# Two projection chunks finished ahead of the scan's norm, pads cleared on GpSimd, norm products between the convolutions

## The chip, the cores and the metric

One core of one Trainium2 chip runs the whole program. The time is the device time of one execution in microseconds (us). A few-word map of the engines in the profile: PE is TensorE (PEld its weight loads), DVE is VectorE, ACT is ScalarE, POOL is GpSimd, SP is SyncE, which issues most of the large loads. All arithmetic is fp32; a matmul with fp32 operands appears in the trace as two matmul instructions.

## What is computed

The reference is two layers of a diffusion backbone over 128 context tokens and 256 latent tokens, width 1024. Layer 0 runs a bidirectional state-space scan beside a gated long convolution (Hyena), layer 1 attention; each is followed by a mixture of 32 experts. The part that matters here is the junction of the two halves of layer 0:

```python
    y, final = bidirectional_ssd(xs, dt_raw, Bm, Cm, A_log, dt_bias, init_state)
    y = y + xs.astype(jnp.float32) * d_skip.astype(jnp.float32)[:, None]
    y = y.astype(h.dtype).reshape(b, L, SSD_INNER)
    y = rmsnorm(y * jax.nn.silu(z), g_ssd)
    parts = jnp.split(dwconv_centred(hy, hy_conv_w, hy_conv_b), 1 + HY_ORDER, axis=-1)
    filters = hyena_filters(L, hy_w1, hy_b1, hy_w2, hy_b2, hy_w3, hy_freq)
    u = parts[0]
    for o in range(HY_ORDER):
        u = parts[o + 1] * long_conv(u, filters[:, o], hy_bias[o])
    return jnp.concatenate([y, u], axis=-1) @ w_out, final
```

`y` is the output of the scan; its norm is over all 1024 channels. `hy` is a projection of 3072 channels, on which a depthwise convolution of three taps is run.

## The kernel before

**Layout and order.** Activations lie with channels on the 128 partitions and 384 tokens (128 + 256) along the row, so 1024 channels are 8 tiles, called chunks. The program has no automatic scheduler: each engine has its own instruction list written by hand, and the engines meet through semaphores. PSUM has 8 banks. The function `bank_plan` (from line 125) lists every bank's use in TensorE's order, with the engine that empties it; `bank_order` deals out the banks in rotation; and `open_bank` (line 840 on) makes TensorE wait until the earlier user of a bank has been emptied. `full(engine, name)` is the other direction: the engine waits until TensorE has completed that entry of the plan. Because both are counts along one list, moving an entry in the plan moves it in all lists.

**The end of the scan.** The scan has 12 steps (`QUADS`). Each ends with a `y` bank, which VectorE (lines 2203 and 2206) adds the skip term to and multiplies into `szT`. To fill TensorE's waits in the scan, the helper `hy_ahead` already issues 14 of the 16 contraction steps of the first two Hyena chunks, (0,0) and (0,1), which sit in banks 7 and 6 and lack only their last contraction step.

**After the scan, in each engine's order:**

- ScalarE squares the 8 chunks of `szT` into `sqssd` (line 1749), waits for TensorE's sum, takes its square root into `rstd` (`root`, line 1592), computes the second set of conditions (`conditions(1)`, line 1641, after the semaphore `const`), and then copies each Hyena chunk from its bank into `hpad`, a row with zero pads, in two pieces (lines 1766 and 1767). There are two `hpad` rows, so chunk c waits for the convolution of chunk c-2 (semaphore `hconv`). The first copy waits for the semaphore `hpad0`, the clearing of the pads.
- TensorE adds up the squares with a matrix of ones (`sum_squares`, 8 matmuls, each after its square), then issues the last contraction step of (0,0) and (0,1), then (0,2), then the filters' first small matmul `f` 0 (which waits for eleven small parameter loads, semaphore `hyc_in`), then (0,3). By the plan's rotation (0,3) uses bank 6, that is the bank of (0,1), which ScalarE must have copied out. Then come two column blocks of the conditioning matrix (`ada`, line 882), (0,4) to (0,6), and so on up to 24 chunks.
- VectorE waits for the root, inverts it (line 2213), forms the 8 norm products `szT` times gain times `rstd` (line 2215, semaphore `yn`), clears the second condition tile (line 2217) and `hpad` (line 2218), and then runs the 24 convolutions (lines 2244, 2245, 2247), with the argument reduction of the filters' sines (`filter_args`, lines 2230 to 2236) after chunks (0,2) and (0,6).
- GpSimd waits for the last `y` bank and issues eleven parameter loads for the filters (lines 2597 to 2604), which go through its own DMA queue, and then nothing until much later.
- SyncE issues the 2 MB weight blocks into a ring of 6 slots; each waits for TensorE's last use of the slot's former block (line 723).

The norm products are read late: ScalarE waits for `yn` before it uses `rstd` for something else, at the last conditioning block (line 1633), and TensorE in `first_states`, in the first turn of the long convolutions.

Of the kernel before, what the change touches and what calls it, by code (L numbers as in the profile page):

```python
# [114 lines left out]
def bank_plan():  # L115
# [3 lines left out]
    def job(name, by, block=None, bank=None):  # L119
        j.append((name, by, block, bank))  # L120
# [42 lines left out]
    for step in range(-1, len(QUADS)):  # L163
# [16 lines left out]
        if step in OFF_AFTER:  # L180
            for g in range(2):
                job(("off", *OFF_AFTER[step], g), "dve")
    job(("ss", "ssd"), "act")

    for q in range(3):
        for c in range(KD):
            job(("hy", q, c), "act", ("hy", q, c // 4) if c % 4 == 3 else None, FILL_BANK[c] if (q, c) in ((0, 0), (0, 1)) else None)
            if ("hy", q, c) in F_AFTER:
                job(("f", F_AFTER[("hy", q, c)]), "dve")
            ada_after(("hy", q, c))  # L190
            if ("hy", q, c) == FILTERS_AFTER:
                for i, (s, x, t) in enumerate(HY_FILTERS):
                    job(("PQ", *HYO[0], s, x, t), "act", None, (7, 6, 1)[i % 3])
            if (q, c) == GATES_AFTER:
                job(("gr", 0), "act")
                job(("gr", 1), "act")
# [228 lines left out]
def build_kernel(nc, A, K, outs):  # L425

    with ExitStack() as ctx:
# [204 lines left out]
        def full(eng, *name):  # L632

            eng.wait_ge(done, JOB[name] + 1)
# [9 lines left out]
        def bank(*name):  # L644
            return banks[BANK[JOB[name]]]
# [192 lines left out]
        def _(pe):  # L838
# [259 lines left out]
            for step in range(-1, len(QUADS)):  # L1098
# [9 lines left out]
                    chunk_state(STATE_AFTER[step])  # L1108
                if step in OFF_AFTER:
                    state_terms(*OFF_AFTER[step])  # L1110
            sum_squares("ssd", sqssd, KD)


            def product(t, h, k):
                act_at = szT[:, k, cols(t)] if k < KD else hyT[:, k - KD, cols(t)]
# [75 lines left out]
            for q in range(3):  # L1191
                for c in range(KD):
                    if c % 4 == 0:
                        arrived(("hy", q, c // 4))
                    if q == 0 and c < 2:
                        open_bank("hy", 0, c)
                        mm(bank("hy", 0, c)[:, 0:T], block_view(("hy", 0, 0))[:, KD - 1, c * P:(c + 1) * P], hT[:, KD - 1, :], False, True)\
                            .then_inc(done, 1)
                    else:
                        project(("hy", q, c), block_view(("hy", q, c // 4)), c % 4 * P, hT)  # L1200
                    if F_AFTER.get(("hy", q, c)) == 0:
                        pe.wait_ge(S("hyc_in"), 16 * 11)
                        ps = open_bank("f", 0)
                        mm(ps[0:HY_HID, 0:T], w1t[0:HY_FEAT, :], featt[0:HY_FEAT, :], True, True).then_inc(done, 1)
                    if F_AFTER.get(("hy", q, c)) == 1:
                        ps = open_bank("f", 1)
                        pe.wait_ge(S("fsin"), 1)
                        mm(ps[:, 0:T], w2t[0:HY_HID, :], h1[0:HY_HID, :], True, True).then_inc(done, 1)
                    ada_after("hy", q, c)
                    if ("hy", q, c) == FILTERS_AFTER:  # L1210
                        pe.wait_ge(S("hs"), 1)
                        pe.wait_ge(S("hypar0_in"), 16 * 6)
                        filters(0, *HYO[0])
                    if (q, c) == GATES_AFTER:
                        for l in range(2):
                            ps = open_bank("gr", l)
                            took(pe, "ada", l, 11)
                            for i in range(4):
                                g, v = divmod(i, 2)
                                last = tr(ps[0:KD, cols(i)], mod[:, l, 16 + 24 * g:24 + 24 * g, v])  # L1220
                            last.then_inc(done, 1)
# [349 lines left out]
        def _(act):  # L1571
# [175 lines left out]
            took(act, "y", NT - 1, 3)  # L1747
            for k in range(KD):
                A_(sqssd[:, k, :], szT[:, k, :], ACT.Square).then_inc(S("sq"), 1)
            root("ssd", D)  # L1750

            def take_filters(turn, b, o):
# [4 lines left out]
            act.wait_ge(S("const"), 2)  # L1757
            conditions(1)
            for c in range(3 * KD):
                if c == 0:  # L1760
                    act.wait_ge(S("hpad0"), 1)
                if c >= 2:
                    act.wait_ge(S("hconv"), c - 1)
                full(act, "hy", c // KD, c % KD)
                ps = bank("hy", c // KD, c % KD)
                A_(hpad[:, c % 2, 1:1 + LP], ps[:, 0:LP], ACT.Copy)
                A_(hpad[:, c % 2, 2 + LP:2 + T], ps[:, LP:T], ACT.Copy).then_inc(taken["act"], 1)  # L1767
                if ("hy", c // KD, c % KD) in F_AFTER:
                    i = F_AFTER[("hy", c // KD, c % KD)]
                    act.wait_ge(S("farg"), i + 1)  # L1770
                    dst = h1[0:HY_HID, :] if i == 0 else hsP
                    src = farg[0:HY_HID, :] if i == 0 else farg
                    A_(dst, src, ACT.Sin).then_inc(S("fsin"), 1)
                ada_after("hy", c // KD, c % KD)
                if ("hy", c // KD, c % KD) == FILTERS_AFTER:
                    act.wait_ge(S("gates_out"), 16 * 2)
                    take_filters(0, *HYO[0])
                if (c // KD, c % KD) == GATES_AFTER:
                    for l in range(2):
                        full(act, "gr", l)  # L1780
                        A_(gstage[0:KD, l, :], bank("gr", l)[0:KD, :], ACT.Copy).then_inc(taken["act"], 1)
                    took(act, "gr", 1)
                    for l in range(2):
                        act.dma_start(gates_d[l].rearrange("g v (c p) -> c (g v) p", p=P),
                                      gstage[0:KD, l, :].rearrange("c (i p) -> c i p", p=P)).then_inc(S("gates_out"), 16)
# [206 lines left out]
        def _(dve):  # L1992
# [218 lines left out]
            took(dve, "y", NT - 1, 3)  # L2211
            took(dve, "ss", "ssd")
            link(nc.vector.reciprocal(rstd, rstd))
            for k in range(KD):
                STT(out=szT[:, k, :], in0=szT[:, k, :], scalar=col("ssd_norm", k), in1=rstd, op0=mult, op1=mult).then_inc(S("yn"), 1)

            nc.vector.memset(conds[1], 0.0).then_inc(S("const"), 1)
            nc.vector.memset(hpad, 0.0).then_inc(S("hpad0"), 1)
            two_pi_hi = float(np.float32(6.28125))
            two_pi_lo = 2.0 * math.pi - two_pi_hi  # L2220
            magic = 12582912.0
# [17 lines left out]
            for c in range(3 * KD):  # L2239
                q, k = divmod(c, KD)  # L2240
                took(dve, "hy", q, k)
                src, acc = hpad[:, c % 2, :], hacc[:, c % 2, 0:n]
                dst = (u0T, p1T, hyT)[q][:, k, :]
                link(TS(acc, src[:, 0:n], col("hy_conv_w", c), col("hy_conv_b", c), mult, add))  # L2244
                link(STT(out=acc, in0=src[:, 1:1 + n], scalar=col("hy_conv_w", 3 * KD + c), in1=acc, op0=mult, op1=add))
                for v, (a, b) in enumerate(SEGS):
                    last = STT(out=dst[:, a:b], in0=src[:, 2 + a + v:2 + b + v], scalar=col("hy_conv_w", 6 * KD + c),
                               in1=acc[:, a + v:b + v], op0=mult, op1=add)
                last.then_inc(S("hconv"), 1)
                if ("hy", q, k) in F_AFTER:  # L2250
                    filter_args(F_AFTER[("hy", q, k)])
                ada_after("hy", q, k)
                if (q, k) == (2, 3):
                    gain(1, 0, "norm_ffn", 32, 11)
                    gain(2, 1, "norm_mix", 8, 11)
                    gain(3, 1, "norm_ffn", 32, 11)
                    dve.wait_ge(S("fsin"), 2)

                    nc.vector.memset(hsP[HY_HID:P, 0:1], 0.0)
                    link(nc.vector.memset(hsP[HY_HID:P, LP:LP + 1], 0.0))  # L2260
                    TS(hsQ, hsP, sgn[:, 0:1], None, mult).then_inc(S("hs"), 1)
# [307 lines left out]
        def _(pool):  # L2569
# [23 lines left out]
                    .then_inc(S("m2"), 1)  # L2593

            full(pool, "y", 2, 3)
            with nc.allow_non_contiguous_dma(reason="a few small parameters"):
                dma(dft, K["k_dft"]).then_inc(S("hyc_in"), 16)
                dma(w1t[0:HY_FEAT, :], A["hy_w1"][0]).then_inc(S("hyc_in"), 16)
                dma(featt[0:HY_FEAT, :], K["k_feat"]).then_inc(S("hyc_in"), 16)
                for j in range(2):  # L2600
                    dma(w2t[0:HY_HID, j * HY_HID:(j + 1) * HY_HID], A["hy_w2"][0]).then_inc(S("hyc_in"), 16)
                for src, c, n in ((A["hy_b1"][0], 0, 1), (A["hy_freq"][0, 0], 1, 1), (A["hy_b2"][0], 2, 2), (A["hy_freq"][0, 1], 3, 2)):
                    for j in range(n):
                        dma(fpar[j * HY_HID:(j + 1) * HY_HID, c:c + 1], src.rearrange("(p o) -> p o", o=1)).then_inc(S("hyc_in"), 16)
# [176 lines left out]
```

## Time and profile before

| | us |
|---|---|
| median of 3 runs | 1398.87 (1397.15 to 1399.19) |
| the profiled execution | 1394.66 |
| its span, first to last instruction | 1392.7 |
| TensorE busy | 1229.0 (88%) |
| VectorE, ScalarE, GpSimd busy | 458.3, 330.3, 190.3 |
| mean granted TensorE clock | 0.950 of full |

The profiled execution took 1394.66 us, 2.0 us more than its span and 4.2 us less than the median of the runs. Start times in the rows further down are counted from the span's start. An entry such as `[2.76 <-ACT arena L1767]` means that the engine stood idle for 2.76 us ahead of this instruction and that the instruction of line 1767 on ScalarE released it. A busy time of merged instructions can overlap the next row by a fraction of a matmul, because matmuls are pipelined.

### The profile page before, as it was taken

Reading aid. Unit: us, or ns where it says so; the run is one execution under the profiler, and the core shown is the slowest. Engines: PE = TensorE matmul, PEld = TensorE weight load, DVE = VectorE, ACT = ScalarE, POOL = GpSimd, SP = SyncE. Lnnn points to the kernel's source line nnn. Section 1 sums busy time; section 2 is a strip of 40 time slices with the busy share of each in tenths; the row PEclk is TensorE's granted clock in tenths of the full one; section 3 lists DMA queues with packets and bytes.
Section 4 is the critical chain, followed back from the end, with each engine's and each line's share of the span. In section 5 each row is a group of like instructions: output and inputs, shape, how many; then the busy total and the mean of one; then the engine's idle time right before and its main releaser. Section 6 shows DMA issues by size and latency. Waiting matters only on the chain.

```text
span 1392.7 us, 16599 instructions
## 1 busy us (share of the span) xinstructions
PE 1229.0 (88%) x6381; PEld 694.0 (50%) x6381; DVE 458.3 (33%) x960; ACT 330.3 (24%) x843; POOL 190.3 (14%) x251
## 2 busy tenths in 40 slices
PE   4999998899989999959999875999888959999774
PEld 2456654455545554446555442753455446555431
DVE  1452078533238850251111113212374241111115
ACT  4112364210022200131111113314353231111113
POOL 1000021100122401011221110152001011112100
PEclk9999999999999999979999997899999979999996
DMA  9895510475920108349999995941312469999993
GB/s 341 318 386 197 181 31 1 179 283 207 363 83 1 61 12 332 120 172 367 419 417 418 420 413 208 372 53 14 136 62 101 183 229 403 418 419 419 419 379 150
DMA packets 94418, 337.25 MB, mean 242 GB/s; under 512 B 12784, under 2 KB 16598, under 8 KB 69649
## 3 DMA queue, kind: packets, MB, share of 16 engines
q1 hardware_dynamic: 73472, 303.18, 55.6%
q0 software_dynamic: 13984, 26.19, 6.7%
q10 hardware_dynamic: 6897, 6.97, 1.5%
q8 instruction: 46, 0.75, 0.2%
q14 instruction: 19, 0.16, 0.0%
HBM read 334.08 MB, written 23.18 MB: 257 GB/s over the span
## 4 chain that ended last, share of the span: by engine, by line
PE 71%; DMA 16%; DVE 6%; ACT 3%; issue 2%; POOL 0%; SPq 0%; ACTq 0%; DVEq 0%; POOLq 0%
PE bank L851 63%; DMA ring<-in_moe_w_down_dram 10%; PE bank L855 5%; DMA ring<-in_moe_w_up_dram 3%; PE bank L882 3%; DMA arena<-expert_rows 1%; DMA xR<-in_x_sample_dram 1%; PE bank L948 1%; ACT ring L1958 1%; DMA hT<-rows,scr 0%; ACT rstd L1598 0%; DVE arena L2471 0%; DVE arena L2474 0%; DMA expert_rows<-arena,scr 0%; DVE arena L2498 0%
## 5 line engine op out<-in xcount | busy, mean ns | idle before, releaser
L851 PE MATMUL bank<-ring,arena 128*64 128x256 f32 (+3 forms) x2624 | 438.5, 439 | 43.6 <-DMA ring<-in_moe_w_up_dram 17.2
L851 PEld LDWEIGHTS bank<-ring,arena 128*64 128x64 f32 (+1 forms) x2624 | 218.3, 146 | 229.8 <-issue 119.9
L851 PE MATMUL bank<-hT,ring 128*128 128x384 f32 (+5 forms) x968 | 310.2, 479 | 7.0 <-ACT hT L1670 3.6
L851 PEld LDWEIGHTS bank<-hT,ring 128*128 128x128 f32 (+1 forms) x968 | 182.9, 196 | 130.1 <-issue 21.1
L851 PE MATMUL bank<-arena 128*64 128x256 f32 (+7 forms) x800 | 117.9, 385 | 10.4 <-DVE arena L2419 4.5
L2446 DVE TENSOR_TENSOR hT<-hT,bank 128x256 f32<-128x256 f32 x32 | 13.5, 421 | 265.8 <-ACT hT L1845 265.8
L851 PEld LDWEIGHTS bank<-arena 128*64 128x64 f32 (+4 forms) x800 | 60.4, 151 | 52.7 <-issue 30.2
L855 PEld LDWEIGHTS bank<-cst,hT 128*128 128x128 f32 x368 | 47.4, 190 | 47.8 <-issue 35.9
L1845 ACT ACTIVATE hT<-bank 128x256 f32<-128x256 f32 x32 | 12.3, 384 | 247.5 <-PE bank L851 247.5
L855 PE MATMUL bank<-cst,hT 128*128 128x128 f32 x368 | 61.0, 301 | 11.1 <-DMA hT<-rows,scr 11.1
L855 PE MATMUL bank<-cst,arena 128*128 128x128 f32 (+3 forms) x207 | 33.3, 312 | 37.5 <-ACT arena L1611 20.0
L851 PE MATMUL bank<-ring,hT 128*128 128x512 f32 x144 | 63.3, 598 | 0.4 <-ACT hT L1972 0.4
L851 PE MATMUL bank<-arena,ring 128*128 128x256 f32 (+3 forms) x272 | 60.0, 373 | 3.2 <-ACT arena L1921 1.8
L2451 DVE COPY arena<-bank 128x512 f32<-128x512 f32 x32 | 22.1, 691 | 111.4 <-PE bank L851 111.4
L851 PEld LDWEIGHTS bank<-arena,ring 128*128 128x128 f32 (+2 forms) x272 | 41.5, 184 | 23.9 <-issue 9.2
L855 PEld LDWEIGHTS bank<-cst,arena 128*128 128x128 f32 (+3 forms) x207 | 27.7, 162 | 48.3 <-issue 39.9
L851 PE MATMUL bank<-arena,cst 128*128 128x512 f32 (+5 forms) x76 | 37.8, 653 | 13.9 <-DVE arena L2392 9.4
L1856 ACT ACTIVATE arena<-bank 128x512 f32<-128x512 f32 x32 | 19.1, 597 | 114.4 <-PE bank L851 114.4
L851 PEld LDWEIGHTS bank<-ring,hT 128*128 128x128 f32 x144 | 27.5, 193 | 34.3 <-issue 33.2
L2667 POOL DMA_INDIRECT hT<-rows,scr x32 | 33.0, 1030 | 70.7 <-PE bank L855 26.8
L2683 POOL COPY scr<-arena 128x1 int32 x28 | 5.1, 183 | 270.5 <-ACT arena L1856 164.2
L2244 DVE TENSOR_SCALAR arena<-arena,par 128x385 f32<-128x385 f32 x24 | 11.6, 482 | 91.4 <-ACT arena L1767 91.4
(305 smaller groups left out, 1141.5 us busy)
## 6 DMA issues: line engine op xcount, KB each, us to landing
ring<-in_moe_w_up_dram SPq DMA_DIRECT2D x28, 2048.0 KB, 20.8
ring<-in_moe_w_down_dram SPq DMA_DIRECT2D x28, 2048.0 KB, 20.0
ring<-in_w_ada_dram SPq DMA_DIRECT2D x24, 2048.0 KB, 14.6
ring<-in_moe_w_gate_dram SPq DMA_DIRECT2D x24, 2048.0 KB, 20.8
ring<-in_ev_w_in_dram SPq DMA_DIRECT2D x11, 2048.0 KB, 11.5
arena<-in_moe_w_gate_dram SPq DMA_DIRECT2D x8, 2048.0 KB, 14.4
ring<-in_ev_w_out_dram SPq DMA_DIRECT2D x4, 2048.0 KB, 15.7
arena<-in_moe_w_up_dram SPq DMA_DIRECT2D x4, 2048.0 KB, 19.1
```

Source lines behind the costliest of these rows:

```text
L851: return nc.tensor.matmul(out, lhsT, rhs, start=start, stop=stop_, skip_group_check=True)
L855: return nc.tensor.transpose(out, in_, ident[0:n, 0:n])
L882: last = nc.tensor.matmul(ps[32 * g:32 * g + 32, :], conds[l][:, k, at:at + 32], w[:, k, :], start=b == first and k < 4, stop=(l, b) in AD ...
L948: last = nc.tensor.matmul(ps[32 * q:32 * q + 32, :], conds[0][:, k, 22 - 2 * j:54 - 2 * j], w[:, k, :], start=j == 0 and k < 4, stop=j == ...
L1845: A_(sg[:, b, :], banks[2 + b][:, 0:HID], ACT.Silu).then_inc(s["silu"], 1)
L1856: A_(ob[:, 0:512], banks[5][:, :], ACT.Copy).then_inc(s["d_act"], 1)
L1958: A_(prob[b][:, a, 0:w], bank("score", n, a)[:, 0:w], ACT.Exp, bias=nrows[:, b, 1, a:a + 1], scale=scale, accum_out=nrows[:, b, 2, a:a + 1 ...
L2244: link(TS(acc, src[:, 0:n], col("hy_conv_w", c), col("hy_conv_b", c), mult, add))
L2446: TT(hid[:, b, :], sg[:, b, :], banks[2 + b][:, HID:2 * HID], mult).then_inc(s["hid"], 1)
L2451: COPY(ob[:, 512:1024], banks[6][:, :]).then_inc(s["d_dve"], 1)
L2667: nc.gpsimd.indirect_dma_start(xs[:, b, :], None, rows_d[l], bass.IndirectOffsetOnAxis(ap=at, axis=0), bounds_check=T - 1, oob_is_err=False)\
L2683: nc.gpsimd.tensor_copy(idxc[:, 2 + b:3 + b], scati[:, bass.ds(n, 1)]).then_inc(S("sidx%d" % l), 1)
```

## The change

The change touches four lists. In the plan and on TensorE, the sum of squares moves from ahead of chunk (0,0) to behind chunk (0,1). On ScalarE, the copies of chunks (0,0) and (0,1) move ahead of the root, after the squares. On VectorE, the two clears are gone and the 8 norm products move behind the first 8 convolutions, one each. On GpSimd, the two clears stand ahead of the eleven parameter loads.

```diff
@@ bank_plan
-    job(("ss", "ssd"), "act")
-
     for q in range(3):
         for c in range(KD):
             job(("hy", q, c), "act", ("hy", q, c // 4) if c % 4 == 3 else None, FILL_BANK[c] if (q, c) in ((0, 0), (0, 1)) else None)
+            if (q, c) == (0, 1):
+                job(("ss", "ssd"), "act")
@@ TensorE
                 if step in OFF_AFTER:
                     state_terms(*OFF_AFTER[step])
-            sum_squares("ssd", sqssd, KD)
-
...
                     else:
                         project(("hy", q, c), block_view(("hy", q, c // 4)), c % 4 * P, hT)
+                    if (q, c) == (0, 1):
+                        sum_squares("ssd", sqssd, KD)
                     if F_AFTER.get(("hy", q, c)) == 0:
                         pe.wait_ge(S("hyc_in"), 16 * 11)
@@ ScalarE
             for k in range(KD):
                 A_(sqssd[:, k, :], szT[:, k, :], ACT.Square).then_inc(S("sq"), 1)
+
+            def pad_chunk(c):
+                full(act, "hy", c // KD, c % KD)
+                ps = bank("hy", c // KD, c % KD)
+                A_(hpad[:, c % 2, 1:1 + LP], ps[:, 0:LP], ACT.Copy)
+                A_(hpad[:, c % 2, 2 + LP:2 + T], ps[:, LP:T], ACT.Copy).then_inc(taken["act"], 1)
+
+            act.wait_ge(S("hpad0"), 1)
+            pad_chunk(0)
+            pad_chunk(1)
             root("ssd", D)
...
             act.wait_ge(S("const"), 2)
             conditions(1)
             for c in range(3 * KD):
-                if c == 0:
-                    act.wait_ge(S("hpad0"), 1)
                 if c >= 2:
                     act.wait_ge(S("hconv"), c - 1)
-                full(act, "hy", c // KD, c % KD)
-                ps = bank("hy", c // KD, c % KD)
-                A_(hpad[:, c % 2, 1:1 + LP], ps[:, 0:LP], ACT.Copy)
-                A_(hpad[:, c % 2, 2 + LP:2 + T], ps[:, LP:T], ACT.Copy).then_inc(taken["act"], 1)
+                    pad_chunk(c)
@@ VectorE
             link(nc.vector.reciprocal(rstd, rstd))
-            for k in range(KD):
+
+            def norm_product(k):
                 STT(out=szT[:, k, :], in0=szT[:, k, :], scalar=col("ssd_norm", k), in1=rstd, op0=mult, op1=mult).then_inc(S("yn"), 1)
 
-            nc.vector.memset(conds[1], 0.0).then_inc(S("const"), 1)
-            nc.vector.memset(hpad, 0.0).then_inc(S("hpad0"), 1)
...
                 last.then_inc(S("hconv"), 1)
+                if c < KD:
+                    norm_product(c)
                 if ("hy", q, k) in F_AFTER:
                     filter_args(F_AFTER[("hy", q, k)])
@@ GpSimd
             full(pool, "y", 2, 3)
+            nc.gpsimd.memset(hpad, 0.0).then_inc(S("hpad0"), 1)
+            nc.gpsimd.memset(conds[1], 0.0).then_inc(S("const"), 1)
             with nc.allow_non_contiguous_dma(reason="a few small parameters"):
                 dma(dft, K["k_dft"]).then_inc(S("hyc_in"), 16)
```

## Rows read from the trace of the kernel before

**Rows 1.** The page: span, and engines' shares of the chain that ended last.

```profile
span 1392.7 us, 16599 instructions
PE 71%; DMA 16%; DVE 6%; ACT 3%; issue 2%; POOL 0%; SPq 0%; ACTq 0%; DVEq 0%; POOLq 0%
```

**Rows 2.** The chain at the junction: start us, us, engine, output, line.

```profile
252.32 2.56 DVE rstd L2213
254.91 4.32 DVE arena L2215 x8
...
259.27 0.42 DVE arena L2217
...
259.80 0.72 DVE arena L2218
...
261.59 8.45 PE bank L851 x16
```

**Rows 3.** TensorE's timeline, 240 to 300 us: start, us, instructions [idle before <-releaser].

```profile
243.98 0.42 PE L851 MATMUL bank<-cst,ring 128*64 128x128 f32 x4
246.20 5.40 PE L851 MATMUL bank<-arena,cst 128*128 128x384 f32 x16 [1.80 <-ACT arena L1749]
251.44 6.61 PE L851 MATMUL bank<-hT,ring 128*128 128x384 f32 x20
257.98 0.86 PE L851 MATMUL bank<-arena 33*64 33x384 f32 x2
261.59 8.45 PE L851 MATMUL bank<-hT,ring 128*128 128x384 f32 x16 [2.76 <-ACT arena L1767]
...
290.06 5.43 PE L851 MATMUL bank<-hT,ring 128*128 128x384 f32 x16
```

**Rows 4.** Windows of 1 us: busy PE, PEld, DVE, ACT, POOL; granted clock; DMA share, GB/s.

```profile
259.00:260.00 1.00, 0.00 (x0) 0.00 (x0) 0.85 (x3) 0.23 (x1) 0.00 (x0) 1.00 0.00 0
...
261.00:262.00 1.00, 0.41 (x1) 0.41 (x2) 0.83 (x2) 0.54 (x3) 0.00 (x0) 0.50 0.00 0
...
268.00:269.00 1.00, 1.00 (x5) 0.60 (x4) 0.93 (x3) 0.00 (x0) 0.00 (x0) 1.00 0.00 0
```

**Rows 5.** ScalarE's timeline, 240 to 300 us.

```profile
245.53 3.41 ACT L1749 ACTIVATE arena<-arena 128x384 f32<-128x384 f32 x8 [5.09 <-DVE arena L2206]
248.96 1.28 ACT L1592 ACT_TABLE_LOAD   x1
...
269.66 0.53 ACT L1773 ACTIVATE arena<-arena 64x384 f32<-64x384 f32 x1 [6.03 <-DVE arena L2236]
```

**Rows 6.** GpSimd's timeline, 240 to 300 us: first and last parameter load.

```profile
244.70 0.60 POOL L2597 DMA_DIRECT2D arena<-in_k_dft_dram  x1 [6.01 <-PE bank L851]
...
249.48 1.09 POOL L2604 DMA_DIRECT2D arena<-in_hy_freq_dram  x2
```

**Rows 7.** GpSimd's groups by line: its clear elsewhere. Busy us, mean ns.

```profile
L2650 POOL MEMSET hT<- 128x2048 f32 x2 | 3.6, 1805 | 66.6 <-PE bank L855 66.6
```

**Rows 8.** Source view of line 2604, the last small loads.

```profile
L2604 POOL DMA_DIRECT2D arena<-in_hy_freq_dram x3: 559/574/579, 247.9 to 250.0; - x3
...
DMA to landing us min/median/max: 6.3/6.7/7.4
```

**Rows 9.** Source view of line 2206: ns min/median/max, first and last start.

```profile
L2206 DVE TENSOR_TENSOR arena<-arena,bank x12: 420/420/421, 187.9 to 245.1; 128x256 f32<-128x256 f32 x12
```

**Rows 10.** VectorE's timeline: first instruction of two later convolutions.

```profile
279.66 0.48 DVE L2244 TENSOR_SCALAR arena<-arena,par 128x385 f32<-128x385 f32 x1 [7.00 <-ACT arena L1767]
...
284.82 0.48 DVE L2244 TENSOR_SCALAR arena<-arena,par 128x385 f32<-128x385 f32 x1 [3.24 <-ACT arena L1767]
```

**Rows 11.** SyncE's waits: us in total, times, longest.

```profile
SPq L770 <- PE bank L851: 362.3, 76, 14.9
```

**Rows 12.** TensorE's timeline, its wait at the end of the projection.

```profile
408.01 2.98 PE L855 MATMUL bank<-cst,arena 128*128 128x128 f32 x12 [2.66 <-DVE arena L2247]
```

**Rows 13.** Window of 1 us behind that wait, columns as in rows 4.

```profile
408.00:409.00 1.00, 0.98 (x5) 0.99 (x6) 0.00 (x0) 0.00 (x0) 0.00 (x0) 0.50 0.00 0
```

## The prediction

> **What bounds the kernel now.** I read the page first: over the whole span TensorE holds 71% of the chain that ended last, DMA 16%, VectorE 6% [rows 1]. So a change at one junction is worth what it gives TensorE there. I then followed the chain through the junction. It leaves TensorE after the sum of squares and runs through the reciprocal (2.56 us), the 8 norm products (4.32), the two clears (0.42 and 0.72), and ScalarE's copies, and comes back to TensorE at 261.59 [rows 2]. TensorE's own timeline says what it did meanwhile: it ended the last `y` at 244.40, waited 1.80 us for the first square, summed until about 251.5, had 20 matmuls and the filters' first two until 258.84, and then stood for 2.76 us until ScalarE's copy of line 1767 freed bank 6 for chunk (0,3) [rows 3]. Of the 10 us of VectorE work TensorE thus feels only the last 2.76.
>
> The third view is the granted clock. It is still full (2.4 GHz) at 259, with TensorE idle, is 0.50 (1.2 GHz) when (0,3) starts, and full again at 268 [rows 4]. The 16 matmuls of (0,3) therefore take 8.45 us, where 16 of the same shape take 5.43 at 290.06 [rows 3]. The wait costs 2.76 and what follows it another 3.02: 5.8 us hang on it.
>
> **The change on TensorE.** The four matmul instructions that complete (0,0) and (0,1) move ahead of the sum. One costs (257.98 - 251.44) / 20 = 0.327 us [rows 3], four 1.31. They need no square, so they lie between 244.40 and 245.7, inside the 1.80 us wait. The sum starts at 246.20 as now, since ScalarE's squares start when VectorE's last product is out, at 245.53 [rows 5]. From 251.44 on 16 instead of 20 remain, then the filters' two: (0,3) could start at 251.44 + 18 x 0.327 = 257.33 instead of 261.59, which is 4.26 earlier.
>
> **Is bank 6 free by then?** ScalarE ends its squares at 248.94 [rows 5]. The two pairs of copies and the hand-over took 260.52 to 261.59, 1.07 us [rows 2], so they now end at 250.0, after (0,1) is complete (245.7) and after the clear of `hpad` (GpSimd may start it at 244.70 [rows 6]). Bank 6 is free 7 us before it is wanted. The root's table load (1.28 us, without a gap behind the squares [rows 5]) moves to 250.0 to 251.3, and the root can still run as the sum ends.
>
> **GpSimd.** It now clears `hpad` (780 elements a partition) and the conditions (432) before eleven loads. Its one clear in the trace took 1805 ns for 2048 elements [rows 7]. In proportion that is 0.69 + 0.38 = 1.07 us, and if most of it were a fixed cost, 3.6 at most. I take 1.1: VectorE needs 1.14 for the same two [rows 2]. Every load behind them is issued that much later. The last one is issued at 250.0 now and lands 6.3 us later [rows 8], at 256.3. The filters' first matmul, which waits for all eleven, would be reached at 251.44 + 16 x 0.327 = 256.67. Now it is reached at 257.98 and nothing shows; the move eats that margin. If the landing shifts by the full 1.1, it comes at 257.4 and TensorE waits 0.75 us. If it does not shift at all (earlier ones took up to 7.4 us, so a part of the time was queueing behind other traffic) the wait is 0. I take 0.5, ends 0 and 0.75, and with clears of 3.6 the landing is at 259.9 and the wait 3.2. That the clear overlaps VectorE's last product costs nothing by the rows: line 2206 took 420 to 421 ns in all 12 steps, beside GpSimd's product or not [rows 9].
>
> **VectorE.** The convolutions start after the reciprocal, near 254.9 instead of 261.13. A convolution takes 5.16 - 3.24 = 1.92 us of each 5.16 us chunk [rows 10]; with a norm product (4.32 / 8 = 0.54 [rows 2]) it is 2.46. Three of them end near 262.3, the argument reduction (about 3.0 us, which ended at 269.66 [rows 5]) near 265.3, then the sine, the copy of (0,3) and its convolution near 269. Chunk (0,4) is complete just ahead of its convolution, which starts at 279.66 [rows 10]; 6.8 earlier is 272.9, so VectorE has caught up by then. Afterwards each norm product sits in 3.24 us of idle time [rows 10]; without that cover the eight would cost 4.3. They end with chunk (0,7), two thirds of the projection before anything waits for them. A convolution is not held up by its own norm product, as `hconv` is raised before it; only the next one is, by 0.54. The second conditions are cleared early, and ScalarE has them by 254, ahead of the conditioning blocks. The banks behind (0,3) were freed in the scan or have a lead of microseconds.
>
> **The clock.** With the wait gone TensorE has at most some 0.5 us of idle between 246 and 270, and I expect full clock through (0,3): 8.45 - 5.43 = 3.02 us. The trace shows another gap of that size at 408.01, 2.66 us long [rows 12], and behind it the clock is 0.50 too [rows 13], so a gap of 2.7 us has cost the clock both times. In the Trainium skill, the page "TensorE: Matmul & The Clock Gate", section "What's actually happening", says that the monitor behind the clock runs freely and is not reset by the kernel's start, so that the same kernel sees its changes at different points in different runs. By that rule the fall behind this gap belongs to some executions of before only, and the sum would be 3.8 us in the others. The rows bear out the fall, and one trace can't show how often.
>
> **The sum**, on the profiled execution: 4.26 (TensorE earlier) - 0.5 (the loads) + 3.02 (clock) = 6.8 us, from 1394.66 to 1387.9. Its time is 4.2 under the median of the runs; taking the same 6.8 off the median gives 1392.1. I carry it through to the end in full: TensorE's timeline shows no wait of a microsecond or more from here to the one at 408.01 [rows 12], and the expert loads, where DMA is on the chain, are released by TensorE itself (76 waits of SyncE at line 770 end on it [rows 11]), so they move along. That wait of 2.66 us stays: what is late there is the last convolution, whose distance from the last chunk is unchanged.
>
> **Rivals.**
> - *Clock gains nothing (0.22).* The fall was absent in most of the timed runs, or comes at another place of the junction, for instance behind the waits at the end of the scan. For: one trace, and GpSimd's loads may leave a small gap. Against: rows 4 and 13. Gain 3.8: 1395.1.
> - *Later falls grow (0.08).* Everything behind comes 7 us earlier, and the falls that follow the waits there (408.01 is one of them) may last longer; one that lasts as long as this one costs 3.0. One or two of them turn 6.8 into 1 to 2.8: 1396.1 to 1398. As likely they shrink, and then it is 1389.
> - *The wait moves to the loads (0.06).* GpSimd's clears take 3.6 us, and the filters' first matmul waits until 259.9. Then 4.26 - 3.2 = 1.1 is gained, and the gap is again long enough for the clock to fall: 1397.8.
> - *Slower (0.03).* The same place beyond its bound: TensorE's first filter matmul and all the projection behind it wait for the eleventh load. It decides when that lands after 261.59 - 0.65 = 260.9, that is 4.6 us later than now; at 7.4 us later (263.7) the kernel is 2.8 slower, 1401.7. For it: GpSimd's queue is slow at small loads. Against it: even the highest bound of the clears is 3.6.
> - *It does not do what it says (0.01).* If a wait that I overlooked held TensorE until VectorE's products, nothing would change.
>
> **The numbers.** The forecast has the remaining 0.60. About 0.2% (2.8 us) is what a measurement of this kernel can tell from no change, so faster means under 1396.1. That holds for the forecast and for nearly all of the first rival (0.19 of 0.22): 0.79. Same is the rest of it, the second and third rivals and the last, with a little for an unlucky median: 0.17. Slower is 0.04, the fourth rival and a tail of the second. The range reaches down to 1389.5 (no wait for the loads, 7.3, and a later fall that shrinks by 2) and up to 1396.8 (the first rival with 1.7 against it); it leaves out about 2 in 10.
>
> **What would show it.** Right: TensorE's chunk (0,3) starts near 257.8 and takes about 5.4 us; the sum of squares still starts near 246.2; ScalarE has four copies between squares and root; GpSimd's two clears take about 1.1 us in all; the granted clock stays 1.00 from 246 to 270. Wrong: a wait of over 1 us ahead of the filters' first matmul, a clock of 0.50 anywhere in the junction, or a chunk (0,4) that waits for ScalarE.

## The result and the profile after

| | before | changed |
|---|---|---|
| median, us | 1396.63 (1391.70 to 1399.19, 13 runs) | 1388.86 (1384.93 to 1392.16, 13 runs) |
| profiled execution / its span | 1394.66 / 1392.7 | 1384.93 / 1382.9 |
| mean granted clock in it | 0.950 | 0.957 |

The ratio is 0.9948, with a 95% interval of 0.9937 to 0.9960: 7.3 us faster, between 5.6 and 8.8. The direction and the size of the forecast (6.8) hold. The predicted time does not: 1388.86 lies 0.6 us under the range, and 3.2 under 1392.1. The kernel before has itself come out 2.2 us below the median of its first three runs. Two executions far outside, one of 4789.86 us (the changed kernel again) and one of 1514.71 us (the kernel before beside it), belong to the slow state and are left out of every ratio below.

TensorE's timeline of the changed kernel, from the last `y` bank on, answers to [rows 3]:

```profile
244.16 0.42 PE L851 MATMUL bank<-cst,ring 128*64 128x128 f32 x4
244.51 1.56 PE L851 MATMUL bank<-hT,ring 128*128 128x384 f32 x4
246.39 5.40 PE L851 MATMUL bank<-arena,cst 128*128 128x384 f32 x16 [0.32 <-ACT arena L1749]
251.62 5.32 PE L851 MATMUL bank<-hT,ring 128*128 128x384 f32 x16
257.71 0.86 PE L851 MATMUL bank<-arena 33*64 33x384 f32 x2 [0.77 <-DMA arena<-in_hy_freq_dram]
258.50 5.43 PE L851 MATMUL bank<-hT,ring 128*128 128x384 f32 x16
263.86 3.64 PE L882 MATMUL bank<-ring,arena 128*32 128x512 f32 x32
```

The four matmul instructions fill the wait ahead of the sum, of which 0.32 us is left. The wait of 2.76 us ahead of (0,3) is gone, a new one of 0.77 us stands ahead of the filters' first matmul, and (0,3) takes 5.43 us instead of 8.45. The windows of the granted clock (columns as in rows 4), of the sum, of (0,3), and of the end of the projection:

```profile
246.00:252.00 6.00, 5.68 (x19) 3.39 (x19) 0.00 (x0) 5.46 (x14) 5.63 (x11) 1.00 0.99 384
258.00:264.00 6.00, 6.00 (x22) 3.10 (x24) 5.79 (x13) 0.00 (x0) 0.00 (x0) 1.00 0.00 0
402.00:406.00 4.00, 2.91 (x15) 1.85 (x16) 0.03 (x1) 1.68 (x3) 0.00 (x0) 1.00 0.00 0
```

ScalarE's timeline answers to [rows 5]:

```profile
249.04 0.26 ACT L1754 ACTIVATE arena<-bank 128x128 f32<-128x128 f32 x1
...
249.62 0.39 ACT L1755 ACTIVATE arena<-bank 128x256 f32<-128x256 f32 x1
250.02 1.28 ACT L1592 ACT_TABLE_LOAD   x1
251.82 0.58 ACT L1592 ACTIVATE rstd<-bank,small 128x384 f32<-128x384 f32 x1 [0.52 <-PE bank L851]
```

The copies end at 250.01, where the sum said 250.0, and the root still waits for TensorE. GpSimd's timeline answers to [rows 6]:

```profile
244.65 0.75 POOL L2602 MEMSET arena<- 128x780 f32 x1 [5.76 <-PE bank L851]
245.33 0.46 POOL L2603 MEMSET arena<- 128x432 f32 x1
245.74 0.61 POOL L2605 DMA_DIRECT2D arena<-in_k_dft_dram  x1
...
250.53 1.10 POOL L2612 DMA_DIRECT2D arena<-in_hy_freq_dram  x2
```

The two clears put the loads 1.04 us later (245.74 for 244.70). VectorE's timeline, two rows of the first turns:

```profile
256.93 0.61 DVE L2221 SCALAR_TENSOR_TENSOR arena<-arena,par,rstd 128x384 f32<-128x384 f32 x1
...
273.54 0.48 DVE L2248 TENSOR_SCALAR arena<-arena,par 128x385 f32<-128x385 f32 x1 [4.88 <-ACT arena L1755]
```

VectorE has its first norm product done by 257.5 and is idle for 4.88 us ahead of the convolution of (0,4).

**Where the time went.** All counts below start at the end of the last `y` bank, 244.40 before and 244.58 after. The conditioning block behind (0,3) starts at 25.58 before (269.98) and 19.28 after: 6.30 us. That stands unchanged 138 us later, where the first transposes start (408.01 and 401.90, 163.61 and 157.32 by this count): 6.29. The spans differ by 9.8 us, and 3.7 of them lie behind that point (984.7 us from the first transposes to the end before, 981.0 after). The program is the same there, and in the twelve profiles of kernels that keep the wait ahead of the transposes this stretch took 981.0 to 986.4 us: 983.0 to 985.2 in the three of the kernel before, 981.0 and 985.1 in the two of the changed one. So the 3.7 us are taken as the execution's own and not as the change's. There the clock falls at other places and for other lengths: at 408 to 412 it was 0.61 on the mean before, while at the same point of the changed kernel, 402 to 406, it stayed 1.00.

### The profile page after: what moved, and what is told of

The parts are those of the page before. It is cut to its first block, busy times and chain, and to the rows that moved or that the text cites. A ratio compares the mean times of both kernels' runs of the same rounds, so it can differ in the third digit from the quotient of the medians.

```text
span 1382.9 us, 16600 instructions
## 1 busy us (share of the span) xinstructions
PE 1221.0 (88%) x6381; PEld 689.0 (50%) x6381; DVE 457.1 (33%) x958; ACT 329.9 (24%) x843; POOL 191.6 (14%) x253
## 4 chain that ended last, share of the span: by engine, by line
PE 71%; DMA 17%; DVE 6%; ACT 3%; issue 2%; POOL 1%; SPq 0%; ACTq 0%; DVEq 0%; POOLq 0%
PE bank L851 63%; DMA ring<-in_moe_w_down_dram 10%; PE bank L855 5%; DMA ring<-in_moe_w_up_dram 3%; PE bank L882 3%; DMA arena<-expert_rows 1%; DMA xR<-in_x_sample_dram 1%; DVE arena L2477 1%; PE bank L948 1%; ACT ring L1963 1%; DVE arena L2480 1%; DMA hT<-rows,scr 0%; DMA arena<-in_hy_freq_dram 0%; ACT rstd L1598 0%; DMA expert_rows<-arena,scr 0%
## 5 line engine op out<-in xcount | busy, mean ns | idle before, releaser
L851 PE MATMUL bank<-hT,ring 128*128 128x384 f32 (+5 forms) x968 | 306.1, 474 | 4.3 <-ACT hT L1670 3.6
L851 PEld LDWEIGHTS bank<-hT,ring 128*128 128x128 f32 (+1 forms) x968 | 180.1, 193 | 125.7 <-issue 19.1
L2681 POOL DMA_INDIRECT expert_rows<-arena,scr x32 | 32.7, 1020 | 59.8 <-POOL scr L2691 23.5
```

Of the source, the lines that this page charges most:

```text
L851: return nc.tensor.matmul(out, lhsT, rhs, start=start, stop=stop_, skip_group_check=True)
L2681: nc.gpsimd.indirect_dma_start(outs_d[l], bass.IndirectOffsetOnAxis(ap=idxc[:, 2 + b:3 + b], axis=0), ob, None, bounds_check=2 * T - 1, oo ...
```

## The experiments

Two numbers are free of what the clock does later on: the time on TensorE from the end of the last `y` bank to the start of (0,3), and to the first transposes at the end of the projection. They are worked out from each timeline. "sum's 16" is the time of the sum's 16 matmul instructions; all times are us. A fall is a stretch in which TensorE's granted clock is 0.50 instead of 1.00. Ratios are to the kernel before, with their 95% intervals.

| kernel | sum's 16 | to (0,3) | (0,3) takes | to the transposes | ratio |
|---|---|---|---|---|---|
| before | 5.40 | 17.19 | 8.45 | 163.61 | |
| before, second and third profile | 5.40 | 17.20, 17.20 | 8.31, 8.41 | 163.48, 163.58 | 1.0000 (0.9987 to 1.0014) |
| changed | 5.40 | 13.92 | 5.43 | 157.32 | 0.9948 (0.9937 to 0.9960) |
| changed, again | 5.40 | 13.58 | 5.43 | 156.98 | 0.9959 (0.9943 to 0.9974) |
| norm products in a block | 5.40 | 13.90 | 5.43 | 157.29 | 0.9952 (0.9935 to 0.9969) |
| clears alone | 7.04 | 16.01 | 5.43 | 159.40 | 0.9953 (0.9938 to 0.9968) |
| norm products alone | 7.01 | 15.98 | 5.43 | 159.38 | 0.9953 (0.9938 to 0.9968) |
| gap filled | 7.04 | 18.84 | 5.43 | 162.24 | 0.9976 (0.9964 to 0.9988) |
| sum first | 6.94 | 15.91 | 5.43 | 159.31 | 0.9951 (0.9932 to 0.9970) |
| table last | 5.40 | 13.08 | 5.43 | 156.48 | 0.9942 (0.9922 to 0.9962) |
| late loads | 5.40 | 14.38 | 5.43 | 157.78 | 0.9956 (0.9939 to 0.9973) |
| early transposes | 5.40 | 13.77 | 5.43 | 154.34 | 0.9926 (0.9906 to 0.9946) |
| table last and early transposes | 5.40 | 13.08 | 5.43 | 153.66 | 0.9909 (0.9893 to 0.9925) |

**Norm products back in a block.** From the changed kernel:

```diff
-                if c < KD:
-                    norm_product(c)
...
+            for k in range(KD):
+                norm_product(k)
             two_pi_hi = float(np.float32(6.28125))
```

> The changed kernel with the 8 norm products back in one block ahead of the convolutions. Theory (TensorE only waits for bank 6, and ScalarE frees that near 250 without VectorE): nothing is lost, TensorE reaches chunk (0,3) near 258.5 as in the changed kernel, granted clock 1.00 through it, 6 to 7.5 us faster than before. Rival (the 4.3 us of norm products off VectorE's way carry the gain): (0,3) starts up to 3 us later, or (0,4) waits for ScalarE, and 3 us or less are left of the gain.

13.90 to (0,3), ratio 0.9952: with the other parts in place, the move of the norm products gives nothing that the profile (0.02 us) or the timed runs show. 4.3 us on VectorE are worth zero here.

**Clears alone.** From the kernel before:

```diff
-            nc.vector.memset(conds[1], 0.0).then_inc(S("const"), 1)
-            nc.vector.memset(hpad, 0.0).then_inc(S("hpad0"), 1)
...
             full(pool, "y", 2, 3)
+            nc.gpsimd.memset(hpad, 0.0).then_inc(S("hpad0"), 1)
+            nc.gpsimd.memset(conds[1], 0.0).then_inc(S("const"), 1)
```

> The kernel before with the two clears on GpSimd and nothing else changed. Theory: ScalarE's copies then wait for neither the clears nor the norm products, since hpad0 was raised behind both; they run right after the conditions, near 253.7 to 254.8, bank 6 is free before TensorE asks for it at 258.84, the gap of 2.76 us and the fall of the clock behind it are gone: 5.8 us faster. The filters' first matmul is reached at 258.0, after the last load has landed (257.6), so it does not wait. Rival (only VectorE's 1.14 us of clears are saved): (0,3) at 260.5, gain 1.1, up to 4.1 if the clock does not fall behind a gap of 1.6 us.

Ratio 0.9953, that is 6.6 us, and (0,3) without a wait. ScalarE's and VectorE's timelines show how: the conditions and the copies follow the root at once, while VectorE is still at its reciprocal (until 257.91), ahead of the norm products.

```profile
255.28 1.28 ACT L1641 ACT_TABLE_LOAD   x1
256.57 0.23 ACT L1641 ACTIVATE arena<-par 128x16 f32<-128x16 f32 x1
256.70 0.26 ACT L1766 ACTIVATE arena<-bank 128x128 f32<-128x128 f32 x1
...
255.36 2.55 DVE L2213 RECIPROCAL rstd<-rstd 128x384 f32<-128x384 f32 x1 [8.46 <-ACT rstd L1592]
257.95 4.32 DVE L2215 SCALAR_TENSOR_TENSOR arena<-arena,par,rstd 128x384 f32<-128x384 f32 x8
```

TensorE's timeline and the window of the same kernel also show what was not expected. The clock fell at another place, behind the 1.80 us wait that this kernel keeps ahead of the sum:

```profile
247.61 7.04 PE L851 MATMUL bank<-arena,cst 128*128 128x384 f32 x16 [1.80 <-ACT arena L1749]
...
261.81 5.43 PE L851 MATMUL bank<-hT,ring 128*128 128x384 f32 x16
```

```profile
247.00:251.00 4.00, 3.39 (x6) 1.91 (x7) 0.00 (x0) 3.98 (x9) 4.00 (x9) 0.57 0.99 336
261.00:267.00 6.00, 6.00 (x19) 3.15 (x18) 5.82 (x13) 0.55 (x2) 0.00 (x0) 1.00 0.00 0
```

16.01 to (0,3) is 14.37 plus the 1.64 that the fall costs, and 17.19 - 14.37 = 2.8, the old wait. In this profile the gain up to the transposes is thus 4.2 us (163.61 less 159.40); the timed runs say 6.6, between 4.5 and 8.7.

**Norm products alone.** From the kernel before:

```diff
-            for k in range(KD):
+
+            def norm_product(k):
...
                 last.then_inc(S("hconv"), 1)
+                if c < KD:
+                    norm_product(c)
```

> The kernel before with the norm products between the convolutions and nothing else changed. Theory: the clears end near 256.0 on VectorE instead of 260.5, bank 6 is free near 257.1, TensorE comes to (0,3) at 258.84 without a wait and at full clock: 5.8 us faster, the same as the clears alone, so that the two parts do not add up. Rival (each part gives its own share of VectorE's time): the block's 4.3 us minus what the clears still cost, a gain that differs from the clears' alone by 3 us.

15.98 and 159.38, ratio 0.9953: within 0.03 us of the clears alone in every column. So both parts remove one and the same wait, and the second one to come adds nothing; the run "sum first" below, which has both, confirms it (15.91, and 0.9951).

**Gap filled.** From the kernel before, four more matmuls ahead of (0,2), whose values its first accumulating step overwrites:

```diff
+                        if (q, c) == (0, 2):
+                            took(pe, *PLAN[PRIOR[JOB[("hy", 0, 2)]]][0])
+                            for _ in range(4):
+                                mm(bank("hy", 0, 2)[:, 0:T], block_view(("hy", 0, 0))[:, 0, 2 * P:3 * P], hT[:, 0, :], True, False)
                         project(("hy", q, c), block_view(("hy", q, c // 4)), c % 4 * P, hT)
```

> The kernel before with four extra matmuls (eight instructions, 2.6 us) at the head of chunk (0,2), which the following start flag overwrites. The wait for bank 6 shrinks to about 0.1 us and (0,3) still starts near 261.6, so only the clock can change. Theory (the idle time made the clock fall): granted clock 1.00 through (0,3), which takes 5.4 instead of 8.45 us, 3.0 us faster than before. Rival (the fall comes from something else in the junction): clock 0.50 as before, no gain or loss.

```profile
246.04 7.04 PE L851 MATMUL bank<-arena,cst 128*128 128x384 f32 x16 [1.80 <-ACT arena L1753]
...
262.04 0.86 PE L851 MATMUL bank<-arena 33*64 33x384 f32 x2
263.07 5.43 PE L851 MATMUL bank<-hT,ring 128*128 128x384 f32 x16 [0.18 <-ACT arena L1771]
```

This kernel does more work and waits for the same copy, and it is 3.4 us faster (1.7 to 5.0). With TensorE busy in place of idle, (0,3) runs at full clock (window 263 to 268: 1.00) and takes 3.02 us less. This execution alone would not settle it: its clock had fallen at the sum instead (7.04 for 5.40), which none of the three profiles of the kernel before shows, and so the gain up to the transposes is only 1.37 us in it. It is the twelve timed runs that carry the reading: without any shortening of the wait for the copy they gain what the sum gave to the clock, 3.0 us.

**The changed kernel again**, unaltered.

> The changed kernel again, unaltered, beside the next three on one chip. Theory: 0.5% faster than before (ratio 0.993 to 0.997), TensorE at chunk (0,3) near 258.5 with a wait of 0.77 us for the last small load ahead of the filters' first matmul, no fall of the clock between 243 and 270 us. Rival (the one profile had luck with the clock): a fall somewhere between 243 and 270 in this profile.

Ratio 0.9959, (0,3) after 13.58 us, a wait of 0.43 us for the loads, no fall between 243 and 270. Its profile shows where an execution's own luck lies: behind the 2.66 us wait at the end of the projection, where the first profile of this kernel kept 1.00, the clock stayed down for 10 us:

```profile
402.00:413.00 11.00, 9.53 (x21) 5.10 (x22) 2.35 (x5) 2.39 (x4) 0.00 (x0) 0.53 0.00 0
```

**Sum first.** From the changed kernel, the sum of squares and the root ahead of (0,0) again:

```diff
+    job(("ss", "ssd"), "act")
     for q in range(3):
...
-            if (q, c) == (0, 1):
-                job(("ss", "ssd"), "act")
...
+            sum_squares("ssd", sqssd, KD)
...
+            root("ssd", D)
             pad_chunk(0)
             pad_chunk(1)
-            root("ssd", D)
```

> The changed kernel with the sum of squares ahead of (0,0) again and the root ahead of ScalarE's first copies; clears on GpSimd and norm products between the convolutions stay. By TensorE's time alone (the term of my sum): four matmuls, 1.31 us, less the 0.77 us wait for the loads that disappears, 0.5 us slower than the changed kernel. Theory from the two one-part kernels: the wait of 1.80 us ahead of the sum is whole again and the clock falls behind it in some executions (0.50 near 246 to 250), which costs another 1.6 us; so 0.5 to 2.1 us slower than the changed kernel, and the sum's 16 matmuls take 7.0 instead of 5.4 us in its profile. Rival: no fall there, 5.4 us.

```profile
245.73 6.94 PE L850 MATMUL bank<-arena,cst 128*128 128x384 f32 x16 [1.81 <-ACT arena L1747]
```

In the profile it is 2.0 us behind the changed kernel at the transposes (159.31 to 157.32): 0.5 by TensorE's own time (15.91 less 1.54 is 14.37, against 13.92), 1.5 by a fall behind the 1.81 us wait. The timed runs do not tell the two kernels apart (0.9951 and 0.9948). So most of the gain does not need the new order of the sum.

**Table last.** From the changed kernel (the two waits for `hyc_in` count to 10 instead of 11):

```diff
-                dma(dft, K["k_dft"]).then_inc(S("hyc_in"), 16)
                 dma(w1t[0:HY_FEAT, :], A["hy_w1"][0]).then_inc(S("hyc_in"), 16)
...
+                dma(dft, K["k_dft"]).then_inc(S("dft_in"), 16)
...
             pe.wait_ge(S("hconv"), 3 * KD)
+            pe.wait_ge(S("dft_in"), 16)
```

> The changed kernel with the 1.28 MB table moved behind the ten small loads in GpSimd's queue, under a semaphore of its own that TensorE waits for only at the end of the projection. Theory (the small loads land late because they are issued behind the clears and queue behind the table's 1.28 MB): the last small one lands before 256.9, the 0.77 us wait ahead of the filters' first matmul is gone, (0,3) at 257.7, 0.8 us faster than the changed kernel, which the timed runs can hardly tell. Rival (the landing is set by something else, such as SyncE's 2 MB block issued at 244.6): the wait stays near 0.8 us or shrinks by at most the 0.6 us of one issue.

The wait ahead of the filters' first matmul is gone, and (0,3) starts after 13.08 us. The source views of the small loads, of the changed kernel and then of this one:

```profile
DMA to landing us min/median/max: 6.6/7.0/7.7
```

```profile
DMA to landing us min/median/max: 4.0/4.4/5.2
```

The last six are issued 0.6 us sooner, counted from the last `y` bank, and take 2.5 to 2.6 us less to land. Of the two candidates the table's 1.28 MB ahead of them in the queue is what kept them; SyncE's 2 MB block is issued 0.03 us behind the last `y` bank in both kernels.

**Late loads.** From the changed kernel, five more clears ahead of the loads:

```diff
+            for i in range(5):
+                nc.gpsimd.memset(conds[1], 0.0).then_inc(S("again"), 1)
+                pool.wait_ge(S("again"), i + 1)
             nc.gpsimd.memset(conds[1], 0.0).then_inc(S("const"), 1)
```

> The changed kernel with the condition tile cleared six times instead of once on GpSimd, which issues the eleven loads some 2.5 us later; this is the place of my slower rival. Theory (the landing moves with the issue): the wait ahead of the filters' first matmul grows from 0.4 to 0.8 to about 3 us, the clock falls behind it (0.50 through most of (0,3)), and 5 to 6 us of the gain are lost, ratio to before 0.998 to 1.001. Rival (the landing is set by the traffic, not by the issue): the wait grows by under 1 us, the clock stays, ratio 0.995 to 0.997.

```profile
258.39 0.86 PE L851 MATMUL bank<-arena 33*64 33x384 f32 x2 [1.23 <-DMA arena<-in_hy_freq_dram]
```

My theory fell, the rival held. The loads are issued 2.8 us later (248.53 for 245.74), the wait grows only by 0.46, the clock stays, the ratio is 0.9956. The landing hardly follows the issue: the small loads land 4.3 us after it at the least here, 6.6 in the changed kernel, although the table is ahead of them in both. The source views say what moved less than the issue: the table landed 7.3 us after its issue here (255.8) and 8.9 in the changed kernel (254.6), and the last small load landed 2.3 and 3.0 us behind it. Why the table takes less time when it is issued later was not tested; SyncE's 2 MB block, issued at 244.83 here and 244.61 there, is in flight at the same time. The slower case of the prediction was further away than it said.

**Early transposes.** From the changed kernel:

```diff
-            pe.wait_ge(S("hconv"), 3 * KD)
+            pe.wait_ge(S("hconv"), KD)
             tokens(*HYO[0])
```

> The changed kernel with one more wait shortened: at the end of the projection TensorE's first transposes wait for the first 8 convolutions, whose output they read, and no longer for all 24. Theory: the wait of 2.66 us near 402 goes, and the fall of the clock behind it, where it occurs, with it (1.4 us): 2.7 to 4 us faster than the changed kernel, 0.7 to 0.8% under before. Rival (what follows needs VectorE behind its last convolution anyway): the wait turns up again a few matmuls later and under 1 us is gained.

```profile
398.99 1.04 PE L855 MATMUL bank<-cst,arena 128*128 128x128 f32 x8
400.35 0.66 PE L855 MATMUL bank<-cst,arena 128*128 128x128 f32 x4 [0.32 <-ACT hT L1795]
401.78 1.10 PE L851 MATMUL bank<-scr,arena 128*128 128x512 f32 x2 [0.78 <-ACT hT L1795]
```

The 2.66 us wait is gone, the transposes start 3.0 us earlier than in the changed kernel (154.34 to 157.32), and the two short waits that follow are the old ones (0.31 and 0.78). Ratio 0.9926. The last convolution now ends beside the transposes (401.02 and 0.75 us), and no wait of TensorE for it shows in the trace.

**Both further edits.** Table last and early transposes in one kernel:

> The changed kernel with both further edits: the 1.28 MB table behind the small loads, and the first transposes waiting for 8 convolutions. Theory (each removes a wait that TensorE itself feels, so here they add): (0,3) starts 13.1 us after the last y bank instead of 13.6 to 13.9, no wait at the end of the projection, ratio to before 0.992 or a little under. Rival (the gain at one place is given back at the next): ratio as for the earlier transposes alone or above, 0.993 or more.

153.66 to the transposes, 3.66 less than the changed kernel, and a ratio of 0.9909 (0.9893 to 0.9925), median 1383.51 against 1396.63. In the profiles the two edits add up (0.84 and 2.98 alone), since each removes a wait of TensorE of its own. The intervals of this kernel and of the changed one do not meet, so it is faster than that. From the early transposes alone (0.9906 to 0.9946) the timed runs do not tell it apart.

**The kernel before, twice more.**

> The kernel before, unaltered, for a second profile. Theory: the clock falls behind the wait of 2.76 us ahead of (0,3), as in the first profile; and as all four profiles that kept the 1.80 us wait ahead of the sum but the first one show, it may fall there too, with the sum's 16 matmuls at 6.9 to 7.0 instead of 5.4 us. If it falls at the sum, the kernel before pays 1.5 us there that my sum did not have. Rival: only the fall ahead of (0,3), as in the first profile.

> The kernel before, unaltered, for a third profile. In the eleven profiles so far the clock falls once or not at all in the second half of the scan: near 213 us in seven, near 246 in the four that kept the 1.80 us wait ahead of the sum and had no fall near 213. Theory (where the fall comes is the execution's own, not the kernel's, and the 1.80 us wait catches it when it has not come near 213): this profile has one of the two and not both; if it is the one near 246, the kernel before is shown to pay 1.5 us there in some executions, and in any case it falls again behind the 2.76 us wait. Rival: the kernel before never falls near 246.

```profile
246.69 5.40 PE L851 MATMUL bank<-arena,cst 128*128 128x384 f32 x16 [1.81 <-ACT arena L1749]
...
262.08 8.41 PE L851 MATMUL bank<-hT,ring 128*128 128x384 f32 x16 [2.76 <-ACT arena L1767]
```

These are the third's rows. In both profiles the clock falls ahead of (0,3), and in neither at the sum. So the fall behind the 2.76 us wait stood in three profiles of three. A cost at the sum in the kernel before, which I had come to expect, was not seen. Both had their earlier fall near 213, so they fit the theory of the third profile without deciding it. (Its count of eleven leaves out two profiles that have no fall in the second half of the scan, those of early transposes and of both further edits.) In timing, eight runs of the kernel before against twenty of the same came out at 1.0000 within 0.14%.

## Why the prediction was right in its mechanism and wrong in its time

- **TensorE's part** (4.26 less 0.5, so 3.76) came out as 17.19 - 13.92 = 3.27. The copies, the sum's start and the 0.327 us matmuls were right. The wait for the loads was 0.77 and not 0.5 (0.27; it is inside the stated ends of 0 and 0.75 but for 0.02), the two filter matmuls and their hand-over took 0.79 and not 0.65 (0.14), and the chunk before them ended 0.1 later. The second profile of the changed kernel, with a wait of 0.43, gave 3.61.
- **The clock's part**, 3.02, came out as 3.02 (8.45 less 5.43). Filling the gap without an earlier copy gave about the same alone (3.4, between 1.7 and 5.0, in timed runs). By the rule that the prediction takes from the Trainium skill, page "TensorE: Matmul & The Clock Gate", section "What's actually happening", a part of the executions should not have had the fall. Three profiles of three had it, so no run here bears that out for this gap. At the end of the projection it is otherwise: twelve profiles have the wait of 2.66 us, and the clock fell behind it in six (all three of before, one of the two of the changed kernel, gap filled, table last). There the rule and the traces agree, for the two profiles of the changed kernel differ; and my sentence that a gap of 2.7 us had cost the clock both times was drawn from too few.
- **The sum**, 6.8, stands against 6.30 at the junction in the profile and 7.3 (5.6 to 8.8) in the timed runs.
- **The step that failed** is "taking the same 6.8 off the median gives 1392.1", and with it the range. The step took the median of three runs as the kernel's time. Thirteen runs, these three among them, had a median of 1396.63, and three later sets of 18 to 20 runs had 1397.15, 1395.71 and 1396.63, so the reference was some 2.2 us high. With 1396.63 the same sum gives 1389.8, 1.0 from the result, and the same range, moved with it, reaches from 1387.3 to 1394.6 and takes the result in. That the three runs lay high was bad luck; that the range took no account of it was the error. What the last 1.0 us are stays open; it lies within the interval of the gain. The prediction itself had the warning, a profiled execution 4.2 us under the median, and it gave the range nothing for it: its lower end took in only a fall behind the change that shrinks.
- **GpSimd's clears** took 0.75 and 0.46, against 0.69 and 0.38 in proportion; the loads moved by 1.04, against 1.1 taken. That the landing would follow the issue was too simple, as late loads and table last show.
- **What the prediction did not see** is that the parts overlap. It said that bank 6 would be free 7 us before it is wanted, and so much lead for a gap of 2.76 is a sign that less would have done. Clears alone and norm products alone each free the bank in time: the copies end at 257.67 with (0,3) at 261.81, and at 259.13 with (0,3) at 260.59. It also said that TensorE feels 2.76 us of 10 us of VectorE's work. The 10 us are the chain from the end of the sum to (0,3); VectorE's share of it is 8.0 (2.56, 4.32, 0.42 and 0.72). No term of the sum hangs on that.
- **The rivals.** That the clock gains nothing is refuted by the gap filled, and that the wait moves to the loads at a price of 3.2 by the 0.77 of the changed kernel. Later falls did differ, in the favourable direction in the first profile.

**Open.** In the second half of the scan each of the 14 profiles has at most one fall: near 213 us in eight (the three of before among them), near 246 in four, none in two. All four near 246 are of kernels that keep the 1.80 us wait ahead of the sum (clears alone, norm products alone, gap filled, sum first). None is of a kernel that fills it. Whether filling that wait saves the changed kernel 1.5 us in some executions is suggested by this and not shown, since the kernel before never fell there. It is open, too, whether a fall near 246 would keep off the one behind the 2.76 us wait: no profile has both a fall near 246 and that wait, so the cost of 3.0 us is shown for executions whose earlier fall came near 213, and for the others only by the mean of the timed runs.

## What to carry to other kernels

Follow the chain back from the engine that is the bound, and ask for its wait which single release ends it: 8.0 us of VectorE's work stood in a chain of 10 us here, TensorE felt 2.76 of them, and moving either of two pieces was enough. Price an idle gap of TensorE with the clock behind it, which more than doubled this one; but read it from several profiles, as behind a wait of 2.66 us it fell in six of twelve. When a time is to be forecast for a kernel whose executions lie 8 us apart, take the reference from many runs, or forecast the difference.

## What was not expected of the hardware

- More work made the kernel faster: 2.6 us of superfluous matmuls ahead of a gap of 2.76 us, which they filled but for 0.18, gave a ratio of 0.9976 (0.9964 to 0.9988).
- Behind gaps of 1.80 us the clock fell in four profiles of seven, at a cost of 1.5 to 1.6 us, without lasting as long as behind the 2.76 us gap (in the clears alone 0.57 over the 4 us from 247 to 251; in the kernel before 0.50 over the 6 us from 261 to 267).
- A switch of ScalarE's function table cost its 1.28 us and nothing besides: the load began 0.01 us behind the last copy (250.02), and in the changed kernel the first activation after the next load (252.42 to 253.70) started at 253.72.
- Small loads on GpSimd's queue landed at the least 6.6 and 6.1 us after their issue behind a 1.28 MB load (the two profiles of the changed kernel), and 4.0 ahead of it. Issued 2.8 us later, behind the same load, they took 4.3, so the time from issue to landing is no property of the small load.
